# Interleaving attention heads with projection blocks, and constant products in the routing waits, in a two-block transformer kernel on one core

## The reference

```python
h = rms_norm_2(x, n1) * (1 + sc1) + sh1
a_b, a_c, a_h, b_v, b_g, c_q, c_k, c_v, d_q, d_k, d_v = split_proj(h @ w_in)
ya = short_conv_mixer(a_b, a_c, a_h, conv_a)          # a_b * dwconv(a_c * a_h)
yb = conformer_conv(b_v, b_g, ...)                    # 31 taps, layer norm, silu
yc = window_attention(rope(c_q), rope(c_k), c_v, kc_c, vc_c, sink)
yd = global_attention(rope(rms(d_q)), rope(rms(d_k)), d_v, kc_d, vc_d)
x_new = x + g1 * (concat([ya, yb, yc, yd]) @ w_out)
h2 = rms_norm_2(x_new, n2) * (1 + sc2) + sh2
x_new = x_new + g2 * expert_choice_ffn(h2, router, w_gate, w_up, w_down)
# expert_choice_ffn: softmax over 16 experts; each expert takes its top 32 tokens,
# runs silu(x @ w_gate) * (x @ w_up) @ w_down and adds gate * y back to those tokens
```

## Time and profile before

| | us |
|---|---|
| median of 3 runs (lowest, highest) | 2448.51 (2446.82, 2451.75) |
| the profiled execution | 2445.71 |
| its span from first to last instruction | 2443.9 |
| TensorE busy | 2180.5 (89%) |
| VectorE busy | 762.3 (31%) |
| ScalarE busy | 623.5 (26%) |
| GpSimd busy | 740.3 (30%) |

### The profile page before, as it was taken

How to read it: one execution, slowest core, us unless ns; L and a number is a source line. 1 busy time by engine, 2 the same in 40 slices (tenths; PEclk the granted TensorE clock), 3 DMA queues, 4 the chain that set the end, 5 groups by cost and what they waited for, 6 DMA issues and landing times.

```text
span 2443.9 us, 32791 instructions
## 1 busy us (share of the span) xinstructions
PE 2180.5 (89%) x13350; PEld 1352.3 (55%) x13350; DVE 762.3 (31%) x1444; ACT 623.5 (26%) x919; POOL 740.3 (30%) x624
## 2 busy tenths in 40 slices
PE   7998999999799999999898999999889885788885
PEld 7876789878687888855543333333257542222221
DVE  4864220122622212374723122222156530010101
ACT  3544333434553334221512000010022410000001
POOL 7655367888194669600200000000010100000000
PEclk9899999999899999999898999999999888999997
DMA  9433769755157786522114899999963169999997
GB/s 296 138 115 127 258 207 317 234 176 175 50 181 256 243 303 233 177 108 78 44 52 199 333 428 429 429 429 429 423 218 139 68 266 423 427 427 429 428 427 290
DMA packets 151380, 635.96 MB, mean 260 GB/s; under 512 B 7816, under 2 KB 14216, under 8 KB 120920
## 3 DMA queue, kind: packets, MB, share of 16 engines
q1 hardware_dynamic: 148224, 623.78, 65.7%
q0 software_dynamic: 2608, 9.25, 1.2%
q10 hardware_dynamic: 424, 1.22, 0.1%
HBM read 633.17 MB, written 1.05 MB: 260 GB/s over the span
## 4 chain that ended last, share of the span: by engine, by line
PE 66%; DMA 19%; DVE 8%; POOL 2%; ACT 2%; issue 2%; SPq 1%; DVEq 0%; ACTq 0%
PE bank L1346 15%; PE bank L622 9%; PE bank L624 9%; PE bank L623 9%; DMA ring<-in_w_up 8%; DMA ring<-in_w_gate 8%; PE bank L1186 4%; PE bank L1309 3%; DMA ring<-in_w_down 3%; PE bank L845 2%; POOL ring_r L1610 2%; PE bank L1195 2%; PE bank L968 2%; PE bank L822 2%; PE bank L834 1%
## 5 line engine op out<-in xcount | busy, mean ns | idle before, releaser
L1346 PE MATMUL bank<-ring,arena 128*32 128x512 f32 x4424 | 649.1, 625 | 129.7 <-DMA ring<-in_w_gate 55.5
L1610 POOL TENSOR_TENSOR ring_r<-ring,ring_r 128x512 fp32r<-128x512 f32 (+1 forms) x468 | 575.2, 1266 | 293.2 <-ACT ring_r L1705 264.5
L1346 PEld LDWEIGHTS bank<-ring,arena 128*32 128x32 f32 x4424 | 192.2, 114 | 561.0 <-issue 536.6
L622 PE MATMUL bank<-ring_r 128*128 128x256 f32 (+1 forms) x1504 | 463.8, 308 | 14.0 <-POOL ring_r L1610 8.3
L624 PE MATMUL bank<-xT_r,ring_r 128*128 128x256 f32 x1248 | 354.4, 284 | 0.0
L623 PE MATMUL bank<-ring_r 128*128 128x256 f32 x1104 | 312.5, 283 | 0.0
L622 PEld LDWEIGHTS bank<-ring_r 128*128 128x128 f32 x1504 | 289.4, 192 | 37.1 <-issue 17.7
L1705 ACT ACTIVATE ring_r<-ring 128x2048 fp32r<-128x2048 f32 (+1 forms) x119 | 216.7, 1828 | 289.1 <-DMA ring<-in_ffn_w_gu 139.2
L624 PEld LDWEIGHTS bank<-xT_r,ring_r 128*128 128x128 f32 x1248 | 239.8, 192 | 0.0
L623 PEld LDWEIGHTS bank<-ring_r 128*128 128x128 f32 x1104 | 211.8, 192 | 0.7 <-issue 0.5
L1639 POOL TENSOR_TENSOR arena<-const 128x1024 f32<-128x1024 f32 x6 | 12.1, 2023 | 646.8 <-DVEq L2233 574.8
(11 more groups left out here) (360 smaller groups left out, 2653.0 us busy)
## 6 DMA issues: line engine op xcount, KB each, us to landing
ring<-in_w_gate SPq DMA_DIRECT2D x52, 2048.0 KB, 17.3
ring<-in_w_up SPq DMA_DIRECT2D x52, 2048.0 KB, 17.3
ring<-in_w_down SPq DMA_DIRECT2D x40, 2048.0 KB, 17.6
ring<-in_ada_w SPq DMA_DIRECT2D x41, 1024.0 KB, 7.5
ring<-in_w_down SPq DMA_DIRECT2D x41, 1024.0 KB, 18.2
ring<-in_ffn_w_gu SPq DMA_DIRECT2D x35, 1024.0 KB, 5.9
ring<-in_w_up SPq DMA_DIRECT2D x18, 1024.0 KB, 8.0
ring<-in_w_gate SPq DMA_DIRECT2D x17, 1024.0 KB, 6.1
```

The costliest lines, as they stand in the source:

```text
L622: pe.matmul(dst, w_hi, v_hi, start=first, stop=False)
L1346: mm = pe.matmul(dst[nb][CAP * b:CAP * b + CAP, :], src[:, c, CAP * b:CAP * b + CAP], rooms[b % G], start=bi_first, stop=bi_last)
L1610: pool.tensor_tensor(lo[:, c], whole[:, c], hi_of(u)[:, c, 0:n], ALU.subtract).then_inc(*signal("w_lo", (u, c)))
```

## The change

The edits, in the order of the file. The second block's weight order, DMA issues and arithmetic stay as they were.

- TensorE, projections: in block ab the order is now chunk ab0, rotations of ck0, dq0, dq1, `turn_conv`, rotation of dk0, chunk ab1, a wait for dk0's rotation on VectorE, the scores of units 0 and 1, chunks ac0 and ac1. The two chunks of block ah are issued behind the values of steps 0 and 1 of the attention. Banks are named anew (`ROT_BANK`, `LATE_BANK`); the two ah chunks and the second `ub` share bank 0.
- ScalarE follows: the copies of ac0, ac1, the two Silus of the long convolution and the copies of ah0, ah1 lie between the exponentials of units 0 to 3.
- VectorE rotates dk0 ahead of the statistics of the long convolution, and waits for ah1 before the output of unit 0. Units 2 and 3 take the arena buffers of 0 and 1 (so their maxima wait for those units' turns); xT serves from unit 4 on.
- Routing: `keep_busy(n)` issues n products of constants (128x128 by 128x512) into bank 7, which nobody reads; 3 ahead of the affinities, 2 while GpSimd makes its second diagonal (layer 0), 4 in layer 1 ahead of the top-32 result, 2 behind `posT`. The last two `rows_hat` go to ScalarE, behind the exponential; TensorE waits for them ahead of the gathers. The clearing of `moe_pick_g` is moved ahead of the wait for `affT`. TensorE's wait for `sel` is gone, GpSimd waits itself.

```diff
@@ helpers
-            return dict(deep=4 if size == 1024 else 2, key=(stage, i), ...
+            return dict(deep=4 if size == 1024 and i not in (2, 3) else 2, key=(stage, i), ...
-            if u["size"] == 1024 and u["n"] % 4 >= 2:
-                m = u["n"] % 4
+            if u["size"] == 1024 and u["n"] >= 4 and u["n"] % 4 < 2:
+                m = u["n"] % 4 + 2
+        ROT_BANK = dict(cq0=6, cq1=7, ck0=6, dq0=7, dq1=4, dk0=5)
+        LATE_BANK = dict(ab0=2, ab1=3, ac0=7, ac1=6, ah0=0, ah1=0)
@@ TensorE
-                    pe.wait_ge(*after("sel", 0))
                         if s < seqs - 1:
                             mm.then_inc(*signal("diag_read", layer))
+                            keep_busy(2)
-                        b = open_bank(("u", layer, tp), 4 + tp)
+                        b = open_bank(("u", layer, tp), tp)
-                    else:
+                    elif blk == "ab":
+                        chunk("ab0", wb, 0)
+                        rotations(("ck0", "dq0", "dq1"))
+                        turn_conv()
+                        rotations(("dk0",))
+                        chunk("ab1", wb, P)
+                        us = block2_units(layer)
+                        pe.wait_ge(*after("rope_out", ("qk", layer, "dk0")))
+                        for u in us[:2]:
+                            scores(u)
+                        chunk("ac0", wb, 2 * P)
+                        chunk("ac1", wb, 3 * P)
+                    elif blk == "b" and layer:
                         for name, at in CHUNKS.items():
-                            if n0 <= at < n1 and (layer, blk) != (0, "b"):
+                            if n0 <= at < n1:
                                 chunk(name, wb, at - n0)
-                        if blk == "ab":
-                            rotations(("ck0", "dq0", "dq1"))
-                            turn_conv()
-                    read(("in2", layer, blk), 2)
-                rotations(("dk0",))
+                    if blk != "ah":
+                        read(("in2", layer, blk), 2)
                 pe.wait_ge(*after("u_norm", (layer, seqs - 1)))
                 for c in range(2):
-                    b = dense_bank(("ub", layer, c))
+                    b = open_bank(("ub", layer, c), (7, 0)[c])
...
-                attend(us)
+                def behind_unit(i):
+
+                    if i < 2:
+                        chunk(f"ah{i}", wb, P * i)
+                    if i == 1:
+                        read(("in2", layer, "ah"), 2)
+                attend(us, behind=behind_unit, scored=2)
...
+                def keep_busy(n):
+
+                    pe.wait_ge(bank_free[7], filled[7])
+                    for _ in range(n):
+                        pe.matmul(bank[7][:, :], con("ones"), con("winmask"), start=True, stop=True)
...
                 route(2 * n_half - 1)
+                keep_busy(3)
                 pe.wait_ge(*after("aff", layer))
...
                 gate_slots()
+                keep_busy(0 if layer == 0 else 4)
                 pe.wait_ge(*after("top", layer))
...
                 mm.then_inc(*filled_now(("posT", layer)))
+                keep_busy(2)
+                for t in tiles[-2:]:
+                    pe.wait_ge(*after("rows_hat", (layer, t)))
@@ GpSimd
-            ins.then_inc(*signal("sel", 0))
+            link(ins)
@@ ScalarE
+                def projections_beside(i):
+
+                    if i < 2:
+                        ab_evac(2 + i)
+                    if i == 1:
+                        conv_out()
+                    if i in (2, 3):
+                        ah_evac(i - 2)
+                for j in range(2):
+                    ab_evac(j)
+                act.wait_ge(*after("uvar", layer))
+                act.activation(std[:, 0:len(tiles)], mv[:, 0:len(tiles), 1], ACT.Sqrt).then_inc(*signal("rstd", ("u", layer)))
+                attend(block2_units(layer), behind_exps=projections_beside)
...
                 act.activation(aff_of(seqs), aff_of(seqs), ACT.Exp).then_inc(*signal("aff_exp", layer))
+                for t in tiles[-2:]:
+                    act.wait_ge(*after("mean_sq", ("root", layer, t)))
+                    act.activation(xhat[:, t, :].rearrange("k (c p) -> k c p", c=KC), x[:, t, :].rearrange("k (p c) -> k c p", c=KC),
+                                   ACT.Identity, scale=rstd[:, t:t + 1]).then_inc(*signal("rows_hat", (layer, t)))
@@ VectorE
+                    if first_output and i == 2:
+                        first_output()
-                rotate(("dq0", "dq1"))
+                rotate(("dq0", "dq1", "dk0"))
...
-                rotate(("dk0",))
-                attend(block2_units(layer), lambda: dve.wait_ge(*after("short", layer)))
+                attend(block2_units(layer), lambda: dve.wait_ge(*after("short", layer)),
+                       first_output=lambda: dve.wait_ge(*full(("c", layer, "ah1"))))
...
                 root_of(L - 1)
-                rows_hat(L - 2)
                 dve.wait_ge(*after("folded", layer))
...
+                if seqs == 2:
+                    dve.memset(moe_pick_g, 0.0)
                 link(dve.memset(ones_row[0:R, :], 1.0))
-                rows_hat(L - 1)
                 dve.wait_ge(*full(key))
...
                 done("top", layer)
-                if seqs == 2:
-                    link(dve.memset(moe_pick_g, 0.0))
```

More of the change, by code:

```diff
@@ L90 @@
           "mods_rows", "mods", "diag", "gates_bc", "u_in", "uconv", "u_norm", "yb", "xhat", "hT", "hT_odd", "aff_exp", "w_hi", "w_lo", "xT_hi", "y_hi", "y_lo", "h_full", "h_hi", "gate_w_hi",
-          "aff", "top", "out_dma", "ab_in", "logit_max", "router_in", "u_in2", "uvar", "ssq2", "short", "ssq_act", "spread", "folded", "x2_half", "xr", "routed", "mean_sq", "diag_read", "sel")
+          "aff", "top", "out_dma", "ab_in", "logit_max", "router_in", "u_in2", "uvar", "ssq2", "short", "ssq_act", "spread", "folded", "x2_half", "xr", "routed", "mean_sq", "diag_read", "rows_hat")
 def weight_plan(w):
@@ L506, in unit @@
         def unit(stage, i, q, k, scale, v, y, keys=256, bias=None, sink_at=None, size=512, parts=None):
-            return dict(deep=4 if size == 1024 else 2, key=(stage, i), n=i, q=q, k=k, scale=scale, v=v, y=y, keys=keys, bias=bias, sink=sink_at, size=size, parts=parts)
+            return dict(deep=4 if size == 1024 and i not in (2, 3) else 2, key=(stage, i), n=i, q=q, k=k, scale=scale, v=v, y=y, keys=keys, bias=bias, sink=sink_at, size=size, parts=parts)
         def half(t, c, j, n0=0, n=SEQ):
@@ L1181, in chunk @@
                 def chunk(name, wb, at, n=n_tok):
-                    b = dense_bank(("c", layer, name))
+                    key = ("c", layer, name)
+                    b = open_bank(key, LATE_BANK[name]) if name in LATE_BANK else dense_bank(key)
                     for c in range(KC):
@@ L1274, in _ @@
                     mm.then_inc(*filled_now(("ub", layer, c)))
-                pe.wait_ge(*after("rope_out", ("qk", layer, "dk0")))
                 pe.wait_ge(*after("proj", ("v2", layer, "cv")))
-                us = block2_units(layer)
-                attend(us)
+                def behind_unit(i):
[4 more added lines that the diff above has]
+                attend(us, behind=behind_unit, scored=2)
                 pe.wait_ge(*after("oT", us[-1]["key"]))
@@ L1804, in evac_T, with attend @@
                 done("probsT", u["key"])
-            def attend(us, between=None, beside=None):
+            def attend(us, between=None, beside=None, behind_exps=None):
                 for i in range(len(us) + 1):
@@ L2147, in _, with ab_evac, ah_evac @@
                 roots(("dk0",))
-                for j, name in enumerate(("ab0", "ab1", "ac0", "ac1")):
-                    evac(("c", layer, name), y_lo[:, j, 0:n_tok])
+                def ab_evac(j):
+                    evac(("c", layer, ("ab0", "ab1", "ac0", "ac1")[j]), y_lo[:, j, 0:n_tok])
                     done("ab_in", (layer, j))
-                act.wait_ge(*after("uvar", layer))
-                act.activation(std[:, 0:len(tiles)], mv[:, 0:len(tiles), 1], ACT.Sqrt).then_inc(*signal("rstd", ("u", layer)))
-                for i in range(2):
+                def ah_evac(i):
                     key = ("c", layer, f"ah{i}")
@@ L2159, in _, with conv_out @@
                     done("ab_in", (layer, 4 + i))
-                act.wait_ge(*full(("ub", layer, 1)))
-                for c in range(2):
-                    key = ("ub", layer, c)
-                    act.wait_ge(*full(key))
-                    at = 2 * layer + c
-                    link(act.activation(yb[:, c, 0:n_tok], bank_of(key)[:, 0:n_tok], ACT.Silu, bias=col("cln_b", at), scale=col("cln_g", at)))
-                    act.sem_inc(*freed(key))
-                    done("yb", (layer, c))
-                attend(block2_units(layer))
+                def conv_out():
+                    act.wait_ge(*full(("ub", layer, 1)))
+                    for c in range(2):
```

(11 more changed lines are left out.)

6 lines of the change are left out of this document (4 added, 2 removed).

## The result

| | before | after |
|---|---|---|
| median (lowest, highest), us | 2447.72 (2446.82, 2451.75), 4 runs | 2422.34 (2421.93, 2423.37), 4 runs |
| ratio after/before, 95% interval | | 0.9895 (0.9874 to 0.9915) |
| the profiled execution; its span | 2445.71; 2443.9 | 2422.65; 2420.8 |

The medians differ by 25.4 us, a gain of 1.05% and just the sum of the forecast (2423, range 2415 to 2433). The two profiled executions differ by 23.1. A stage that was not edited and whose clock was the same repeats to 0.1 us or so from profile to profile, so the comparison is made by stages. Two stretches do not repeat so well: the expert loops, and the start up to the first ab chunk (1110.5 to 1118.1 us in 13 of the 14 profiles, 1129.3 in one).

The account below looks back on a forecast made before the run. TensorE, idle and partly at half clock, was taken to bound the stretches ahead of the DMA-bound expert loops. 13.4 + 3.6 + 3.9 + 4.5 = 25.4 us, taken from the median, gave 2423 us (2418 to 2428; whole range 2415 to 2433).

Parts of the forecast that it names:

- Layer 0, attention: Layer 0, first ab chunk to end of attention: 14.9 us won less 0.8 and 0.7, so 13.4 (bounds 9 and 15).
- the wait behind `short`: Layer 0's attention: TensorE gets a bank 0.8 us late, as unit 4's output waits for GpSimd's chain.
- GpSimd beside VectorE: Layer 0's attention: GpSimd's chain slows VectorE's normalise pairs beside it; 0.7 us taken, bounds 0 and 3.4.
- Layer 0, routing: Layer 0's routing: `posT`'s copy 2.1 us earlier and the gather 1.75 shorter, sum 3.9 us (bounds 2 and 5.5).
- Layer 1, attention: Layer 1's attention: 5.1 us won despite three new idle times, less 1.5 for half clock, so 3.6 (bounds 0 and 5).
- Layer 1, routing: Layer 1's routing: experts start at 1990.3 instead of 1994.87, 4.5 us won (bounds 2 and 5).
- case (C): Rival, both routings: clock not held and constant products stand in the way, 1.72 us each; 2442.5 us, chance 0.08.
- Expert loops: Expert loops of both layers: as long as before; an earlier first group starts the DMA stream equally earlier.
- (A): Rival: layer 1's interleaving gives nothing, eaten by three new idle times and the clock; 2427 us, chance 0.14.
- (B): Rival: bank 0 slower, ScalarE's exponential pairs precede each ah0 and ah1 copy, 9.2 us in both layers; 2432, chance 0.06.
- (D): Rival: loads ahead of the experts rule their start and eat all the gain; 2448.5 us, chance 0.06.
- (E): Rival: slower, GpSimd's chain stretches beside dense units and VectorE queues behind it; sign turns at factor 1.9; 2458, chance 0.06.

Follow-up runs that it names:

- short_two: Changed kernel with GpSimd's short convolution cut to two of its 14 operations, both layers: layer 0's attention 107.77 us against 109.16, median 2425.0 us.
- final: The kernel `combined` plus the two narrow constant products of `early` and an earlier start of GpSimd's short convolution: median 2419.8 us, ratio 0.9879.
- rows_dve: Changed kernel with the last two row scalings back on VectorE: layer 0's routing 23.82 us against 21.83, median 2424.4 us, ratio 0.9919.
- no_products: Changed kernel with all four `keep_busy` calls removed: layer 0's routing 26.34 us against 21.83, layer 1's 20.06 against 19.00, median 2427.4 us.
- gap: Changed kernel with three more constant products ahead of layer 0's first expert product: layer 0's routing 23.36 us, its experts 533.8, median 2426.2 us.
- order1: Changed kernel with another order of chunks, rotations and scores in layer 1's attention: that stage 70.87 us against 74.88, median 2423.9 us.
- combined: Changed kernel with the order of `order1`, ac0 and ac1 in banks 6 and 7, two products ahead of the affinities, and the products of `gap`: median 2415.5 us.
- routing: Kernel before with the routing edits alone: layer 0's routing 21.83 us, layer 1's 17.30, median 2440.8 us, ratio 0.9973.
- attention: Changed kernel with every routing edit undone: attention 109.16 us in layer 0 and 74.91 in layer 1, median 2427.8 us, ratio 0.9918.
- early: Changed kernel with one 256-column constant product ahead of the last router transposes and one ahead of the last router products: layer 1's routing 17.21 us, median 2434.1 (one run).

## Why the prediction was right, and where not

In this section "on the old axis" means times of the profile after, shifted so that the stage starts where it did before.

**Layer 0, attention (13.4, measured 13.4): right, with one deduction out of two in the wrong place.** The order of events came as written: no wait over 0.2 us up to unit 0's turn, clock 1.00. I deducted 0.8 for the wait behind `short` and 0.7 for GpSimd beside VectorE. `short_two` gives 1.39 for both, all of it the wait: that 0.8 and 0.7 add up to nearly as much is luck. The contention is real in single rows (0.88 to 1.99) and costs nothing on the path of this kernel; in `final` it reaches the path, with 0.50. The Trainium skill, GPSIMD Engine Reference, section Specifications, says that GpSimd shares its SBUF interfaces with VectorE, and these rows agree. The 2.7 us less that the full price of the contention would have made of the sum did not come. The sign that I had named for a wrong forecast, unit 4's output waiting over 3 us, did appear (3.24): it was a badly chosen sign, for VectorE comes there 1.9 us ahead of TensorE's need, and TensorE lost 1.37.

**Layer 0, routing (3.9, measured 3.9): right.** On the old axis `posT` begins at 1311.4, as forecast, and the gather takes 3.65 us (3.6). `rows_dve` gives the row scalings 2.0, `no_products` the products 4.5; together more than the gain, because with the clock already lost one hides part of the other. The clock held in seven of the nine kernels with these products and without the narrow ones (not in `gap` and `rows_dve`), and the fall in `gap` cost 1.5: so the sum was right for the likelier case.

**Layer 1, attention (3.6, measured 1.8): the mechanism right, the clock's term too small.** On the old axis dk0's rotation waits 3.2 us (3.4 forecast), the scores begin at 1877.8 (1877.8), ah0 at 1895.3 (1895.0), its wait and the unforeseen one for bank 6 (ac1 lies in the bank of the turn) are 3.2 together where I had one of 2.9. The wait of 2.1 ahead of the scores did not come, because ab1 ran at half clock in that time. Then ah0 takes 6.23 instead of 3.72: 2.5 us where I had put 1.5 for the whole stage. Another 0.7 are spread over the steps up to unit 1's values (1914.7, forecast 1911.5 before the clock's deduction). The waits were mine to remove: order1 and combined take 4.0 and 5.5 us out of this stage.

**Layer 1, routing (4.5, measured 2.9): the step that failed is `keep_busy(3)` ending ahead of the affinities.** At full clock it does, and `routing` alone gives 4.6. In the changed kernel the clock fell before the first of the products had begun, which no number of products behind that point can prevent, and at half clock they lasted so long that the transposes came 1.8 us after the affinities. The forecast named this as a sign that it is wrong, and it is a part of case (C): the clock is not always held, and then the products stand in the way.

**Expert loops (0): right within their scatter.** x0 is 0.7 longer, x1 2.5 shorter. A longer expert loop was a third sign of being wrong, but over all profiles x0 ranges from 532.3 to 538.8. That a faster first group shortens the whole loop is supported by `gap`, `combined` and `final`.

**The rivals.** (A) was nearest: layer 1's interleaving alone gives 1.8. (B) did not occur (0.19 and 1.69 us at bank 0). (D) is ruled out by all stages. (E) holds as a mechanism, and steeper than I wrote, 1.3 us per microsecond in layer 0 instead of 1; but the chain took 21.2 us against 20.9, a factor of 1.01 where 1.9 was needed.

## What to carry to other kernels

Price an interleaving by the idle time it removes plus the half clock behind it, and then price each new wait the same way: here such waits cost themselves and 2.0 to 2.5 us of slow work after them. Products of constants that fill a wait must be fewer than the wait holds at half clock, or they turn from cover into delay. Give banks in the order in which the engines free them, and compare stages, not totals, when a change is 1% and one execution differs from the next by as much.

## What the runs showed of the hardware

**The clock can fall while TensorE is busy without a break.** In layer 1's routing it fell in eight of nine kernels that had the constant products without the narrow ones, for 3.4 us or (`gap`, `short_two`) 6.8, and TensorE's only idle times just before were of 0.26 to 0.56 us, among transposes and products of 16 columns. It fell 0.35 to 1.6 us after the start of the last router products, in six of the eight before the first constant product began; `attention` and `no_products`, which have none, show the same fall (0.9 and 0.4 us after that start). So the constant products did not bring it about. In layer 0 it fell beside them in two kernels: in `gap` at 1294.4, 0.7 us after the first had begun. With a narrow product in each of these waits it fell in none of four routings (`early`, `final`). Only layer 1's two tell much, for layer 0's clock held in seven of nine kernels without them. That these short waits decide is thus supported and not shown, and why `routing` alone was spared isn't settled. The Trainium skill, TensorE: Matmul & The Clock Gate, section "A second HAM failure mode: psum-queue depth-cycling", tells of a bf16 kernel whose short, frequent idle times between groups of products make the clock swing. These float32 runs are compatible with that.

**An activation that reads SBUF in permuted order took nearly twice as long.** ScalarE's scaling of 128x1024 float32, two of them in one row, and the final one, the same function with a scale for each partition but read in order:

```profile
1291.00 4.21 ACT L2236 ACTIVATE arena<-x,rstd 128x1024 f32<-128x1024 f32 x2
...
2415.13 1.15 ACT L2271 ACTIVATE x<-arena,rstd 128x1024 f32<-128x1024 f32 x1 [0.36 <-DVEq L2284]
```

That is 2.1 us each against 1.15; VectorE's in permuted order takes 1.15 too.
